# Local attention steps: low and high part of the turned weights directly behind logits and ahead of exponentials; sums and result parts last

## What is computed

```
q, k, v: 16 query heads in 4 groups share 4 key/value heads, width 64
blocks of 128 queries see their own, the previous and the next block of 128 keys
logits = q k^T / 8 + bias[head, key - query], masked to |key - query| <= 128
m = max(max(logits), sink[head])
p = exp(logits - m);  p = p / (sum(p) + exp(sink - m))
out = p v
```

## Time and profile before

| | |
|---|---|
| median of 3 runs | 1905.18 us (1903.18 to 1905.78) |
| the profiled execution's own time | 1901.99 us |
| its span, first to last instruction | 1900.1 us |
| PE busy | 1851.0 us, 97% |
| DVE, ACT, POOL busy | 923.5, 757.5, 1365.9 us |
| local attention steps, 0 to 63 | about 558 to 719 us of the span |
| mean granted TensorE clock | 0.997 |

### The profile page before, as it was taken

The page is one execution under the profiler, slowest core; times in us unless marked ns, Lnnn a source line. Parts: engine busy times, 40 slices in busy tenths (PEclk is TensorE's granted clock), DMA queues, the critical chain, the costliest instruction groups (busy, mean ns, idle before and its releaser), DMA issues.

```text
span 1900.1 us, 26191 instructions
## 1 busy us (share of the span) xinstructions
PE 1851.0 (97%) x9597; PEld 1562.1 (82%) x9597; DVE 923.5 (49%) x1829; ACT 757.5 (40%) x1431; POOL 1365.9 (72%) x1211
## 2 busy tenths in 40 slices
PE   7999999999998899999999999999999999999999
PEld 6888888888877777888888888897679888888887
DVE  6677777762038875345503421727652455203410
ACT  4677777654026673142101210568643522101100
POOL 8766666798844458979988988753434679888985
PEclk9999999999999999999999999999998999999999
DMA  7322222223332222423333233221122222333332
GB/s 224 106 67 67 67 67 67 67 67 111 111 94 62 60 74 89 137 75 93 95 91 109 89 93 106 67 66 63 38 74 89 90 67 89 89 106 93 88 107 70
DMA packets 213614, 165.71 MB, mean 87 GB/s; under 512 B 14479, under 2 KB 209874, under 8 KB 213123
## 3 DMA queue, kind: packets, MB, share of 16 engines
q1 hardware_dynamic: 208134, 149.32, 26.9%
q10 hardware_dynamic: 5372, 14.98, 2.4%
HBM read 161.11 MB, written 7.37 MB: 89 GB/s over the span
## 4 chain that ended last, share of the span: by engine, by line
PE 81%; POOL 6%; issue 3%; DVE 3%; PEld 3%; ACT 2%; PEldq 0%; DMA 0%; ACTq 0%; POOLq 0%; DVEq 0%; SPq 0%
PE bank L401 55%; PE bank L483 9%; POOL w_lo L3220 4%; PEld bank L401 2%; PE bank L451 1%; POOL w_hi L3212 1%; PE bank L427 1%; PE bank L1247 1%; PE bank L1584 1%; PE bank L1791 1%; PE bank L1193 1%; PE bank L1244 1%; PE bank L1802 1%; PE bank L1781 1%; PE bank L2970 1%
## 5 line engine op out<-in xcount | busy, mean ns | idle before, releaser
L3220 POOL TENSOR_TENSOR w_lo<-w_raw,w_hi 128x512 fp32r<-128x512 f32 (+1 forms) x572 | 718.2, 1286 | 207.8 <-ACT w_hi L1431 198.4
L3212 POOL TENSOR_TENSOR w_hi<-w_raw,one 128x512 fp32r<-128x512 f32 (+1 forms) x428 | 442.0, 1063 | 238.9 <-PE bank L401 215.5
L401 PE MATMUL bank<-h_hi,w_hi 128*128 128x512 f32 x952 | 381.3, 401 | 1.1 <-POOL w_lo L3220 0.8
L401 PE MATMUL bank<-h_hi,w_lo 128*128 128x512 f32 x952 | 372.0, 391 | 0.0
L401 PE MATMUL bank<-h_lo,w_hi 128*128 128x512 f32 x952 | 371.1, 390 | 0.0
L401 PE MATMUL bank<-a_hi,w_hi 128*128 128x512 f32 x832 | 326.0, 392 | 1.6 <-POOL w_lo L3220 1.3
L401 PE MATMUL bank<-a_hi,w_lo 128*128 128x512 f32 x832 | 324.0, 389 | 0.0
L401 PE MATMUL bank<-a_lo,w_hi 128*128 128x512 f32 x832 | 323.8, 389 | 0.0
L401 PEld LDWEIGHTS bank<-h_hi,w_lo 128*128 128x128 f32 x952 | 178.7, 188 | 38.6
L401 PEld LDWEIGHTS bank<-h_hi,w_hi 128*128 128x128 f32 x952 | 178.9, 188 | 36.0 <-issue 1.4
L401 PEld LDWEIGHTS bank<-h_lo,w_hi 128*128 128x128 f32 x952 | 179.2, 188 | 34.3
(11 more groups left out here) (502 smaller groups left out, 3029.1 us busy)
## 6 DMA issues: line engine op xcount, KB each, us to landing
w_raw<-in_w_ff SPq DMA_DIRECT2D x32, 1024.0 KB, 5.5
w_raw<-in_w_in SPq DMA_DIRECT2D x31, 1024.0 KB, 5.4
w_raw<-in_w_mlp_in SPq DMA_DIRECT2D x16, 1024.0 KB, 5.4
w_raw<-in_w_mlp_out SPq DMA_DIRECT2D x16, 1024.0 KB, 5.6
w_raw<-in_w_in SPq DMA_DIRECT2D x26, 512.0 KB, 4.4
w_raw<-in_w_ssd_out SPq DMA_DIRECT2D x8, 1024.0 KB, 6.0
bias_rows<-bias_row ACTq DMA_DIRECT2D x1, 4096.0 KB, 15.6
w_raw<-in_w_attn_out SPq DMA_DIRECT2D x4, 1024.0 KB, 5.4
```

The source lines that it names most:

```text
L401: mm = pe.matmul(bank[:, 0:ntok], a, b[:, koff + k, 0:ntok], start=(k == 0 and n == 0), stop=(k == L.kb - 1 and n == 2))
L3212: pool.tensor_tensor(w_hi[:, slot, part], raw[:, slot, part], one[:].broadcast_to([P, n]), ALU.mult).then_inc(split_hi, 1)
L3220: ins = pool.tensor_tensor(w_lo[:, slot, part], raw[:, slot, part], w_hi[:, slot, part].bitcast(F32), ALU.subtract)
```

## The change

In `window_attn_act`, `high(u - 3)` and `probs(u)` move ahead of `below` and `out_high`, and stand directly behind the hooks. In `window_attn_dve`, `low(u - 3)` moves directly behind `logits(u)`, ahead of `normed_weights(u - 1)`, `summed` and `out_low`. Hooks, waits, tiles and PE's list are as before.

```
@@ window_attn_act @@
             for u in range(ALL_UNITS + WEIGH_AT - REP + 3):
                 at_step(hooks, u)
+                if 3 <= u < ALL_UNITS + 3:
+                    high(u - 3)
+                if u < ALL_UNITS:
+                    probs(u)
                 if u > WEIGH_AT and u % REP == 1:
                     below((u - WEIGH_AT) // REP)
                 if u > WEIGH_AT and u % REP == 2:
                     out_high((u - WEIGH_AT) // REP)
-                if 3 <= u < ALL_UNITS + 3:
-                    high(u - 3)
-                if u < ALL_UNITS:
-                    probs(u)
@@ window_attn_dve @@
                 at_step(hooks, u)
                 if u < ALL_UNITS:
                     logits(u)
+                if 3 <= u < ALL_UNITS + 3:
+                    low(u - 3)
                 if 1 <= u < ALL_UNITS + 1:
                     normed_weights(u - 1)
                 if u > WEIGH_AT and u % REP == 1:
                     summed((u - WEIGH_AT) // REP)
                 if u > WEIGH_AT and u % REP == 2:
                     out_low((u - WEIGH_AT) // REP)
-                if 3 <= u < ALL_UNITS + 3:
-                    low(u - 3)
```

More of the change, by code:

```diff
@@ L1933, in window_attn_act @@
                     out_high((u - WEIGH_AT) // REP)
[L1934 to L1937, removed]
         def window_attn_dve(dve, hooks):
```

## The result

The changed kernel takes 1907.53 us (median of 20 runs, 1905.91 to 1912.47), the kernel before in the same runs 1904.45 (20 runs, 1901.95 to 1906.61). The ratio is 1.0018 with the interval [1.0011, 1.0025], so the change costs 2 to 5 us. The profiled execution took 1908.1 us, its span is 1906.2 at a mean granted clock of 0.996.

A forecast was written before the change was run, and what follows sets the result against it. PE and DVE, nearly equally loaded, were taken to hold each other up. Terms -0.44 + 1.1 + 1.4 - 0.6 = +1.5, plus 0.9, gave +2.4 us: profiled 1901.99 becomes 1904.4, 3.19 under the median, so 1907.5; range 1899.0 to 1912.5.

The forecast's parts named there:

- the accumulator's read: On DVE, the low part may have to wait for this 0.08 us read; 0.9 us taken for some 30 steps.
- Stalls trade places: Rival three and the forecast itself: the order doesn't matter, stalls only trade places, +0 to +3 us, chance 0.5.
- The new waits: DVE's sums wait 0.46 to 0.59 us for ACT's copied half, the result's low part 0.27 to 0.40, in most rounds.
- The bound of 12 us: New idle time on DVE at most: 14 rounds up to step 63 at 0.86 us each.
- what it adds: Part listing the change's costs: ACT's copies follow the exponential, so DVE's sums and result's low part wait for them.
- the signs: Expected in the profile: PE's waits 12 to 20 us, DVE waits of 0.5 and 0.3, POOL's split at 720 to 722.
- The round that was worked through: Steps 20 to 24 laid out in the new order: step 22 gains 0.68 us, the round costs 0.1 more.
- The first and the last rounds: Steps 3 to 20 were to gain 0.44 us, the last rounds up to step 63 0.6 us.
- Behind step 63 nothing is added: Up to L427's products at 728.58: PE idles up to 0.4 us, the last transposes come some 0.5 later relative to POOL's start.
- The rule against the row: POOL's split at 719.19: by the skill's port rule the sum is 1 to 2 us higher; by the row it doesn't grow.
- Rival 1: The new waits fall into time DVE idles for scores, so only the gain is left: 1899.3 us, chance 0.2.
- Rival 2: DVE becomes the bound and each new wait moves everything: +6 us, 1911.3, split behind 724, chance 0.3.

The follow-up runs named there:

- e3: Changed kernel with ACT's order high part, result's copies, exponential: 1902.53 us, ratio 0.9994 against the kernel before.
- e6: Changed kernel with DVE's low part behind the scaling but ahead of the sums, and ACT's result's copies between high part and exponential: 1894.57 us, ratio 0.9955.
- e10: e6 with ACT's list as in the changed kernel, the result's copies behind the exponential: 1903.06 us, ratio 1.0000 against the kernel before.
- e2: ACT's part of the change alone, DVE's list as in the kernel before: 1929.03 us, ratio 1.0139 against the kernel before.
- e7: e6 with DVE's low parts of the queries two steps later: 1906.30 us, ratio 1.0014 against the kernel before.
- e8: e3 with DVE's scaling ahead of the low part in every fourth step, and the queries' low parts two steps later: 1905.55 us, ratio 1.0014.

## Why the prediction was right, point by point

The forecast was 1907.5 and the median is 1907.53. That it is so close is chance. The runs of this kernel spread over 6 us, and terms were off in both directions. The forecast also started from 1905.18, while the kernel before took 1904.45 in these runs: what was forecast is a change of 2.4 us, and what was measured is 3.1 (3.4 by the ratio). A term of the forecast, 0.9 us for the accumulator's read, turned out to be nothing; without it the change would have been put at 1.5. What can be compared is the distance between transposes in the two timelines. Before, those of steps 3, 20, 28, 32, 36 and 52 start at 563.82, 606.89, 628.45, 639.11, 648.84 and 689.88, POOL's split at 719.19 and L427 at 728.58; after the change at 564.83, 607.92, 629.88, 641.40, 651.06, 693.89, 723.20 and 733.67. The change of each distance:

| stretch | forecast | measured |
|---|---|---|
| steps 3 to 20 | -0.44 | +0.02 |
| 20 to 22 | -0.68 | -0.70 |
| 20 to 23 | +0.29 | +0.28 |
| 20 to 24 | +0.10 | +0.08 |
| 20 to 28 | +0.12 | +0.40 |
| 28 to 32 | +0.99 | +0.86 |
| 32 to 36 | 0 | -0.07 |
| 36 to 52 | +1.4 | +1.79 |
| 52 to POOL's split | -0.6 | 0.00 |
| split to the products of L427 | 0 | +1.08 |
| all, without 20 to 22, 23 and 24 | +1.5 | +4.1 |

The span is 6.1 us longer in these two executions: 4.1 in the stage, 1.0 ahead of it and 1.0 behind it. The medians differ by 3.1. The 1.0 on either side is not due to the change. The same instructions stand there in every kernel, and in all ten experiments the transposes of step 3 start at 564.4 to 565.8 and it is 1170.6 to 1173.4 us from L427's first product to the end, against 563.82 and 1171.5 before and 564.83 and 1172.5 after the change. In the profiled execution of the kernel before step 3 merely came early, and its time is 2.5 us under its median.

- **Stalls trade places: right.** The round that was worked through came out to 0.02 us at three points: the stall of step 22 all but gone, sums waiting 0.53 us (I had 0.46 to 0.59), step 23 late.
- **The new waits: right in place, too large in size, and the largest was not named.** The sums wait in 12 rounds of 14, 4.3 us in all, about 0.36 each and not 0.5. The result's low part waits in 5 rounds, 1.0 us in all, not in most and not 0.3. The bound of 12 us became 5.3. That they cost at all is shown by e3, without them and 4.6 us faster. DVE's wait for the high part grew most, from 3.2 to 16.5 us. The round that was worked through has it, in step 20, but it is neither under "what it adds" nor among the signs; e3 against e6 puts 7.4 us on the scaling's place, from which this wait comes, and the changed kernel against e10 3.4.
- **The accumulator's read: the 0.9 us were not there.** The low part starts at 612.54 in the same instant as the read, and what stands behind the read does so in 40 of the 64 steps; in most of the others the low part waits for the high part.
- **The first and the last rounds: the gain was too large.** Up to the transposes of step 10 the kernel gained 1.51 us, by step 12 0.70 of it was left, and by step 20 nothing, where the forecast had 0.44. The last rounds gained nothing, where it had 0.6.
- **The result's low part had the wrong duration.** I laid it out at 0.34 us from its start to the next. That fits the kernel before, where a row's duration is 0.42 each time (in this round at 582.42), with the next operation 0.33 to 0.39 behind its start. In the new order 12 of the 14 up to step 63 fall beside POOL's splits:

```profile
584.46 1.09 DVE L1980 TENSOR_TENSOR a_lo<-arena,a_hi 128x256 fp32r<-128x256 f32 x1
```

The busy time of this line by form, of 558 to 722 (count, busy us, mean ns, idle before), after:

```profile
L1980 DVE TENSOR_TENSOR a_lo<-arena,a_hi 128x256 fp32r<-128x256 f32 x13 | 9.6, 738 | 1.1 <-ACT a_hi L1926 1.0
```

and before:

```profile
L1980 DVE TENSOR_TENSOR a_lo<-arena,a_hi 128x256 fp32r<-128x256 f32 x14 | 5.9, 420 | 0.0
```

That is 0.32 us more each, about 4 us in the stage, on an engine that has little room. In turn the scalings of 384 columns got shorter, from 20.8 us in 32 to 18.4. In steps 20 to 28 the result's low parts are 0.8 us longer and the scalings 0.6 shorter. I had looked at what POOL's split does to scalings, and not at the other DVE operation whose operands lie in no bank. What these longer operations cost by themselves was not tried. That they make up the difference of steps 36 to 52, where the scalings are as long as before, is argued from the rows; for steps 20 to 28 it stays open. They don't decide between the orders: e3 has 14 of them beside a split, 12.3 us in all, and is faster than the changed kernel.

- **"Behind step 63 nothing is added": wrong, by 1.08 us.** The timeline of POOL, DVE and PE from the split on, in place of the earlier trace rows:

```profile
723.20 4.26 POOL L3212 TENSOR_TENSOR w_hi<-w_raw,one 128x512 fp32r<-128x512 f32 x4 [5.46 <-PE bank L401]
...
723.55 0.84 DVE L1959 TENSOR_SCALAR arena<-arena,small 128x256 f32<-128x256 f32 x1
...
724.31 1.26 DVE L1980 TENSOR_TENSOR a_lo<-arena,a_hi 128x256 fp32r<-128x256 f32 x1
...
726.51 0.41 PE L1791 MATMUL bank<-ident,arena 128*128 128x128 f32 x2 [1.11 <-DVE arena_rounded L1966]
...
733.67 0.40 PE L427 MATMUL bank<-a_hi,w_hi 128*128 128x512 f32 x1
```

The transposes at 726.51 are 3.31 us behind the start of the split; the same ones before were at 720.88, 1.69 behind 719.19. I had put them 0.5 later. They are 1.62 later, more than the slack of 0.4, so PE, and no longer POOL, is last at L427: the chain of waits has PE's own work ahead of it, where the earlier trace rows has POOL's split.

```profile
731.52 1.38 PE bank L401 x6
732.90 0.93 PE bank L1802 x4
733.83 10.93 PE bank L427 x48
```

In e6 the split starts at 711.37 and L427 at 720.99, 9.62 behind, and POOL is last again.

- **The rule against the row: the row held, nearly.** POOL's split grew from 4.16 to 4.26 us with three slow DVE operations beside it (0.84, 1.26 and 1.14), 0.1 and not the 1 to 2 by which the rule's sum was higher. It is DVE that lost 0.5 to 0.8 us for each. POOL does lose when DVE is first: in e6 a result's low part starts at 711.33, 0.04 ahead of the split, and takes 0.41; the split takes 4.38, its first operation 1.28 instead of 1.04. The Trainium skill (Advanced Engine Details and Errata, VectorE Performance Modes) says that GpSimd's instructions and VectorE's two-port ones block each other. The scalings' rows agree with that on DVE's side, and on POOL's by 0.1 to 0.2 us a split. The table of that section of the Trainium skill gives a tensor-tensor operation no two-port mode. The rows go beyond it: L1980 is slowed all the same.
- **Rivals.** Rival 1 (waits covered) fell: the sums wait, and PE's waits did not drop under 8 us. Rival 2 (DVE becomes the bound, split behind 724) was near: DVE's idle time ahead of the logits fell from 21.4 to about 4 us, and the split is at 723.20, where my sign was 720 to 722; 1.0 of it is from ahead of the stage. So the split lies between my sign and the rival's, or at the edge of mine without that 1.0, and the measured time is my forecast's.

What the prediction lacked altogether is the view of single moves. It treated the change as one thing with one gain, and did not ask which of the moves in it pays; the table of orders shows that +3 us is made of moves each worth several us, up to 14.

## What to carry to other kernels

When an order of work in two lists is changed, lay out each instruction moved past another as its own edit, and try them singly: here, with ACT's list as before, the low part ahead of the sums gained 6.5 us, and moving it ahead of the scaling as well lost 13.7. An instruction that waits for another engine should have work that is ready standing ahead of it; what is put ahead of the wait must not itself wait. A copy that others need should not stand behind an exponential that waits for its step's logits, and an operation with no operand in a bank that is moved to a time when POOL works has to be given its duration there, not elsewhere.

## What the runs showed of the hardware

- A tensor-tensor operation of DVE with both operands outside the banks (L1980, 128x256) takes 0.42 us alone. When POOL's tensor-tensor operations already run at its start it takes up to 1.26 (0.53 to 1.26 in the changed kernel; a few, at the end of a split in other kernels, 0.41 to 0.49). When it starts first it keeps its 0.41 to 0.43, and POOL's first operation is the longer one: in e6 0.87 us at 594.91, where it was 0.62 at 595.32 in the kernel before. An operation with one operand in a bank (L1966, 128x384) took 0.55 at 629.19 in the changed kernel, beside POOL as well. The four operations of 128x512 of POOL's L3212 took 4.15 to 4.38 us.
- The granted clock fell to 0.50 behind stalls of PE of 1.92, 2.49 and 2.52 us (e2), 2.05, 2.15, 2.48 and 2.50 (e7), 3.03 and 3.04 (e8), and stayed at 1.00 behind others of 1.87 and 1.95 us (e2), 2.05 (e7) and 2.18 (e8). At 0.50 three transposes took 0.87 us instead of 0.52. Stalls up to 1.2 us, in e10, left it at 1.00 throughout the stage.
- A DVE operation that doesn't use the accumulator's value starts in the same instant as the read of the accumulator (612.54), so the read, 0.08 us in its row, costs it nothing.
